# The second block's first eight rotations: halves swapped and summed by TensorE

## The reference, cut to what matters

```python
def rope(x, pos):
    half = x.shape[-1] // 2
    ...
    x1, x2 = xf[..., :half], xf[..., half:]
    return jnp.concatenate([x1 * cos - x2 * sin, x1 * sin + x2 * cos], axis=-1).astype(x.dtype)

qa = rope(qa.reshape(bsz, L, A_HEADS, HEAD_DIM), positions)   # 512 columns: rotations 4 to 7
ka = rope(ka[:, :, None, :], positions)[:, :, 0]              # rotation 3
qi = rope(qi.reshape(bsz, L, IDX_HEADS, IDX_DIM), positions)  # 256 columns: rotations 0 and 1
ki = rope(ki[:, :, None, :], positions)[:, :, 0]              # rotation 2
o_a = dsa_attention(qa, ka, va, qi, ki, wi)

# in dsa_attention, for a block of queries:
idx_logit = jax.nn.relu(jnp.einsum('bthd,bsd->bths', _rows(qi, t0), ki))
score = jnp.einsum('bth,bths->bts', _rows(wi, t0), idx_logit)
_, sel = lax.top_k(score, k_sel)                              # 256 keys, then softmax attention over them
```

## Time and profile before

| | |
|---|---|
| median of 3 runs | 2726.5 us (2716.0 to 2730.44) |
| profiled execution | 2723.89 us, its span 2722.0 us |
| busy share of the span | TensorE 87%, VectorE 62%, ScalarE 48%, GpSimd 31% |
| mean granted clock of TensorE | 0.933 of full |
| chain that ended last | TensorE 52%, VectorE 23%, ScalarE 11%, GpSimd 6%, issue 5% |
| 1 MB chunks of `in_w_in` | 5.5 us from issue to landing (median of 14) |

### The profile page before, as it was taken

One profiled execution on the slowest core, in us unless ns is written; L12 is line 12 of the kernel. 1 busy time (PEld: TensorE's weight loads), 2 busy tenths in 40 slices (PEclk: granted clock), 3 DMA queues, 4 the chain that ended last, 5 costly groups with the idle time before them and its releaser, 6 DMA issues.

```text
span 2722.0 us, 38617 instructions
## 1 busy us (share of the span) xinstructions
PE 2378.0 (87%) x15899; PEld 2119.0 (78%) x15899; DVE 1695.0 (62%) x2589; ACT 1309.9 (48%) x2133; POOL 849.3 (31%) x519
## 2 busy tenths in 40 slices
PE   4999997888899999999998886888887874999994
PEld 3999997888899889899897775667666763877773
DVE  3445545778843766666666657846566425888885
ACT  3444333344433556565565343542344212888884
POOL 1211114455431222222221124213010113776672
PEclk8999997899999999999998998898898976999997
DMA  4232420111052222222222323124111432888773
GB/s 145 78 93 79 129 78 32 32 32 32 13 143 71 64 78 79 71 75 65 76 67 55 88 64 92 47 65 115 39 43 41 126 104 90 290 284 288 277 265 146
DMA packets 228329, 275.54 MB, mean 101 GB/s; under 512 B 42792, under 2 KB 194953, under 8 KB 215482
## 3 DMA queue, kind: packets, MB, share of 16 engines
q1 hardware_dynamic: 213642, 264.64, 31.1%
q0 software_dynamic: 14512, 8.45, 1.0%
HBM read 283.24 MB, written 31.05 MB: 115 GB/s over the span
## 4 chain that ended last, share of the span: by engine, by line
PE 52%; DVE 23%; ACT 11%; POOL 6%; issue 5%; DMA 2%; SPq 1%; DVEq 0%; POOLq 0%; ACTq 0%
PE ps L92 16%; PE ps L94 14%; PE ps L93 14%; ACT whi L98 2%; DVE prods L1143 2%; DVE wlo L102 2%; ACT sp L114 1%; PE ps L1819 1%; DVE fsum L970 1%; DVE work L2682 1%; POOL wlo L102 1%; DVE m L2680 1%; DVE p L2114 1%; ACT X L114 1%; PE ps L1829 1%
## 5 line engine op out<-in xcount | busy, mean ns | idle before, releaser
L92 PE MATMUL ps<-hn_h,whi 128*128 128x264 f32 (+2 forms) x2256 | 691.6, 307 | 39.3 <-POOL wlo L102 30.0
L93 PE MATMUL ps<-hn_l,whi 128*128 128x264 f32 (+2 forms) x2256 | 674.3, 299 | 0.0
L94 PE MATMUL ps<-hn_h,wlo 128*128 128x264 f32 (+2 forms) x2256 | 674.0, 299 | 0.0
L92 PEld LDWEIGHTS ps<-hn_h,whi 128*128 128x128 f32 x2256 | 431.1, 191 | 68.4 <-issue 37.3
L94 PEld LDWEIGHTS ps<-hn_h,wlo 128*128 128x128 f32 x2256 | 431.1, 191 | 12.5
L93 PEld LDWEIGHTS ps<-hn_l,whi 128*128 128x128 f32 x2256 | 431.3, 191 | 9.5
L102 POOL TENSOR_TENSOR wlo<-wraw,whi 128x2048 fp32r<-128x2048 f32 (+1 forms) x48 | 176.8, 3683 | 508.1 <-ACT whi L98 508.1
L98 ACT ACTIVATE whi<-wraw 128x2048 fp32r<-128x2048 f32 (+1 forms) x164 | 260.1, 1586 | 64.8 <-PE ps L94 64.5
L102 DVE TENSOR_TENSOR wlo<-wraw,whi 128x2048 fp32r<-128x2048 f32 (+1 forms) x116 | 244.5, 2108 | 49.0 <-ACT whi L98 48.9
L730 DVE SCALAR_TENSOR_TENSOR c<-ub,vec,c 128x528 f32<-128x528 f32 x48 | 45.3, 943 | 140.1 <-ACT c L114 140.0
L114 ACT ACTIVATE ub<-ps,vec 128x528 f32<-128x528 f32 x48 | 33.7, 702 | 165.1 <-PE ps L94 165.1
(11 more groups left out here) (766 smaller groups left out, 6778.8 us busy)
## 6 DMA issues: line engine op xcount, KB each, us to landing
wraw<-in_w_gate_up SPq DMA_DIRECT2D x33, 1024.0 KB, 7.5
wraw<-in_hy_w_in SPq DMA_DIRECT2D x32, 1024.0 KB, 5.8
wraw<-in_da_w_in SPq DMA_DIRECT2D x64, 512.0 KB, 4.3
ex_raw<-in_w_gate_up SPq DMA_DIRECT2D x31, 1024.0 KB, 6.4
ex_raw<-in_w_down SPq DMA_DIRECT2D x17, 1024.0 KB, 6.0
wraw<-in_w_down SPq DMA_DIRECT2D x15, 1024.0 KB, 7.5
wraw<-in_w_in SPq DMA_DIRECT2D x14, 1024.0 KB, 5.5
wraw<-in_hy_w_out SPq DMA_DIRECT2D x8, 1024.0 KB, 8.5
```

Source lines behind the costliest of these rows:

```text
L92: e.matmul(out, lhsT=l[0], rhs=r[0], start=start, stop=False)
L93: e.matmul(out, lhsT=l[0], rhs=r[1], start=False, stop=False)
L94: return e.matmul(out, lhsT=l[1], rhs=r[0], start=False, stop=stop)
```

## The change

The three last weight chunks of the group change places: qa0 comes before ki. GpSimd splits ki and the last three gate chunks; VectorE splits qa0, ka, qa1 and the first gate chunk. For rotations 0 to 7 ScalarE's copy, the swaps by transfer and GpSimd's products are gone. VectorE reads the bank twice and writes the products with cosines and with sines (`vector_parts`); TensorE adds them in the same bank with two float32 matmuls, one with the identity and one with a matrix that swaps the halves and turns the sign (`tensor_rotation`). High and low parts of 3 to 7 are made from the bank; 0 to 2 are multiplied by the norm out of the bank. Turns 0 to 2 stand inside projection 4, the others behind projections in `MIX`. Banks are free when a rotation's low part is done. The index scores have five banks and not six. Rotations 8 to 13 stay.

```diff
     plan("vgw", cols(mw, (576, 640, 0), (2216, 2240, 64), (928, 936, 88)))
     plan("qi", wk(mw, (640, 896)))
+    plan("qa0", wk(mw, (0, 256)))
     plan("ki", cols(mw, *[(896, 928, 32 * i) for i in range(4)]))
     plan("ka", cols(mw, (512, 576, 0), (512, 576, 64)))
-    plan("qa0", wk(mw, (0, 256)))
     plan("qa1", wk(mw, (256, 512)))
...
-        pool = i in even_slots if i >= EX else i % 3 == 0 and i != DAO + 1 or first["gate", "a", 0] <= i < first["cmp"]
+        pool = i in even_slots if i >= EX else i % 3 == 0 and i != DAO + 1
+        if first["vgw"] <= i < first["cmp"]:
+            pool = i == first["ki"] or i > first["gate", "a", 0]
         return ("w.lo.pool", i) if pool and not gathered(i) else ("w.lo.vec", i)
...
+        for i, g in enumerate((32, 16)):
+            to, by = (x.rearrange("p (a h r) -> p a h r", h=2, r=g) for x in (swaps[:, i, :], ident[:]))
+            for h in range(2):
+                ts(e, to[:, :, h, :], by[:, :, 1 - h, :], -1.0, None, ALU.mult).then_inc(*mark("dao.pool", "swaps"))
         for m in range(8):
             lo_weights(e, w, "pool", first["dao", m] + 1 if m < 7 else first["ki"])
...
     def left(w, x):
 
-        w.wait_ge("px.act" if x < 9 else "px.vec", "left", x)
+        if x == 0:
+            w.wait_ge("px.act", "left", 0)
+        elif x < 9:
+            w.wait_ge("px.vec", "turned", PX[x][2])
+        else:
+            w.wait_ge("px.vec", "left", x)
 
     def px_bank(x):
-        return bank[3 + x] if x < 3 else bank[(x + 1) % 2]
+        return bank[3 + x] if x < 3 else bank[x % 3] if x < 9 else bank[(x + 1) % 2]
...
     def tensor_project(e, w, x):
-        if x == 4:
-            w.wait_ge("dao.vec", "evicted", 7, 0)
+        if x < 6:
+            w.wait_ge("dao.vec", "evicted", 7, x - 4)
+        elif x < 9:
+            left(w, x - 3)
+        elif x < 11:
+            w.wait_ge("at.act", "exp", 14, 1)
         else:
             left(w, x - 2)
-        if x in (9, 10):
-            w.wait_ge("at.act", "exp", 14, 1)
         for k in range(8):
             if (x, k) == (4, 0):
                 w.wait_ge("n2.vec", "acc")
                 w.wait_ge("n2.pool", "acc")
                 tensor_columns(e, sq8b[:, 0], range(4)).then_inc(*mark("n2.pe", "sum"))
-            if (x, k) == (4, 3):
+            if x == 4 and k in (3, 5, 6):
+                tensor_rotation(e, w, k // 2 - 1 if k < 6 else 2)
+            if (x, k) == (4, 4):
                 w.wait_ge("n2.vec", "r")
                 tensor_along(e, bank[7], by_n2, range(4)).then_inc(*mark("n2.pe", "r"))
             tensor_project_part(e, w, x, k)
 
+    def vector_parts(e, w, rot):
+
+        x = rotated_at[rot]
+        hi, lo, tab, scale, _ = ROT[rot]
+        came(w, x)
+        if rot < 3:
+            tables_there(w)
+        else:
+            w.wait_ge("n2.vec", "table", tab + 1)
+        if rot >= 4:
+            w.wait_ge("px.pe", "turn", rot - 4)
+        for i, y in enumerate(turning(rot)):
+            t = (tabs if rot < 3 else tabs_r)[:, tab + i, :]
+            e.scalar_tensor_tensor(y[:], px_bank(x), scale, t, ALU.mult, ALU.mult).then_inc(*mark("px.vec", "parts", rot))
+
+    def tensor_rotation(e, w, rot):
+        b = px_bank(rotated_at[rot])
+        c, s = turning(rot)
+        w.wait_ge("px.vec", "parts", rot)
+        w.wait_ge("dao.pool", "swaps")
+        e.matmul(b, lhsT=ident[:], rhs=c[:], start=True, stop=False)
+        e.matmul(b, lhsT=swaps[:, ROT[rot][2] // 2, :], rhs=s[:], start=False, stop=True).then_inc(*mark("px.pe", "turn", rot))
...
     def scalar_project(e, w, x):
         name, c, rot, over = PX[x]
-        b = px_bank(x)
         if x > 3:
             scalar_weights(e, w, first[name] + 1)
-        if x < 9:
+        if x == 0:
             came(w, x)
-        if x == 0:
-            act(e, vg[0:96, :], b[0:96], ACT.Copy).then_inc(*mark("px.act", "left", x))
-        elif x < 9:
-            turning_free(w, rot, "turned")
-            act(e, turning(rot)[0][:], b, ACT.Copy, scale=ROT[rot][3]).then_inc(*mark("px.act", "left", x))
-        elif rot is not None and ROT[rot][4]:
+            act(e, vg[0:96, :], px_bank(0)[0:96], ACT.Copy).then_inc(*mark("px.act", "left", x))
+        elif x > 9 and rot is not None and ROT[rot][4]:
...
     def scalar_rotated(e, w, rot):
-        w.wait_ge("px.vec", "rotated", rot)
+        if 3 <= rot < 8:
+            w.wait_ge("px.pe", "turn", rot)
+            src = px_bank(rotated_at[rot])
+        else:
+            w.wait_ge("px.vec", "rotated", rot)
+            src = turning(rot)[0][:]
...
-        elif rot is not None:
-            g = 32 if ROT[rot][2] == 0 else 16
-            r, s, _ = turning(rot)
+        elif rot is not None and rot >= 8:
+            r, s = turning(rot)
             left(w, x)
-            turning_free(w, rot, "rotated")
-            for j in range(128 // g):
-                e.dma_start(s[g * j:g * j + g, :], r[g * (j ^ 1):g * (j ^ 1) + g, :]).then_inc(*land(f"rot{rot % 4}", rot))
...
     def vector_rotated(e, w, rot):
         hi, lo = ROT[rot][0:2]
-        r, s, _ = turning(rot)
+        r, s = turning(rot)
+        b = px_bank(rotated_at[rot])
         if rot < 3:
-            w.wait_ge("px.vec", "sum", rot)
+            w.wait_ge("px.pe", "turn", rot)
             w.wait_ge("n2.act", "r")
-            e.scalar_tensor_tensor(r[:], r[:], 1.0, rr2[:], ALU.mult, ALU.mult).then_inc(*mark("px.vec", "rotated", rot))
-        else:
+            e.tensor_tensor(r[:], b, rr2[:], ALU.mult).then_inc(*mark("px.vec", "rotated", rot))
+        elif rot >= 8:
             w.wait_ge("px.pool", rot)
             add(e, r[:], r[:], s[:]).then_inc(*mark("px.vec", "rotated", rot))
         w.wait_ge("px.act", "turned", rot)
-        lo_sum(e, lo, r[:], hi).then_inc(*mark("px.vec", "turned", rot))
+        if 3 <= rot < 8:
+            lo_part(e, lo, b, hi).then_inc(*mark("px.vec", "turned", rot))
+        else:
+            lo_sum(e, lo, r[:], hi).then_inc(*mark("px.vec", "turned", rot))
...
     def index_bank(i, h):
-        return bank[2 + (8 * i - 8 + h) % 6][:, 0:128 * (i + 1)]
+        return bank[3 + (8 * i - 8 + h) % 5][:, 0:128 * (i + 1)]
...
-    MIX = [("px", 4), ("first", 0), ("first", 1), ("rot", 0), ("vg",), ("px", 5), ("first", 2), ("rot", 1), ("rot", 2), ("tables",),
-           ("px", 6), ("ix", 1, 0), ("ix", 1, 1), ("rot", 3), ("px", 7), ("rot", 4), ("ix", 2, 0), ("ix", 2, 1), ("px", 8), ("rot", 5),
-           ("ix", 3, 0), ("ix", 3, 1), ("rot", 6), ("rot", 7)]
+    MIX = [("px", 4), ("vg",), ("rot", 0), ("rot", 1), ("rot", 2), ("tables",), ("parts", 3), ("ix", 1, 0), ("ix", 1, 1),
+           ("px", 5), ("turn", 3), ("rot", 3), ("parts", 4), ("px", 6), ("turn", 4), ("rot", 4), ("ix", 2, 0), ("ix", 2, 1), ("parts", 5),
+           ("px", 7), ("turn", 5), ("rot", 5), ("ix", 3, 0), ("ix", 3, 1), ("parts", 6), ("px", 8), ("turn", 6), ("rot", 6), ("parts", 7),
+           ("turn", 7), ("rot", 7)]
 
     def sync_mix(e, w):
-        for x in range(1, 4):
-            sync_project(e, w, x)
...
@@ -2752,11 +2782,8 @@
                     scalar_p1_root(e, w, 1)
                 if (z, k) == (0, 4):
                     scalar_weights(e, w, first["ka"])
-                if (z, k) == (1, 3):
-                    scalar_weights(e, w, first["qa0"])
+        scalar_project(e, w, 0)
         scalar_weights(e, w, first["qa1"])
-        for x in range(4):
-            scalar_project(e, w, x)
...
         mix_tree(e, w, "n2.vec", 1, add)
+        vector_parts(e, w, 0)
         w.wait_ge("n2.act", "sqrt")
         e.reciprocal(by_n2, by_n2).then_inc(*mark("n2.vec", "r"))
-        lo_weights(e, w, "vec", first["qa0"])
+        vector_parts(e, w, 1)
+        vector_parts(e, w, 2)
+        lo_weights(e, w, "vec", first["qa1"])
...
     def gpsimd_mix(e, w):
         mix_tree(e, w, "n2.pool", 0, lambda e, out, a, b: e.tensor_tensor(out, a, b, ALU.add))
-        lo_weights(e, w, "pool", first["qa1"])
-        for x in range(1, 4):
-            gpsimd_project(e, w, x)
         for kind, *of in MIX:
             if kind == "px":
...
+            w.wait_ge("px.vec", "turned", 3)
             w.wait_ge("px.vec", "turned", 4 + a)
             w.wait_ge("ix.act", 3, 7)
             mask = selb[:, i - 1, 0:nk] if i else trir[:]
@@ -2939,7 +2967,9 @@
             w.wait_ge("px.vec", "turned", 12 if z == "slc" else 13)
             mask = trir[:]
         if n == 0:
+            left(w, 6)
             left(w, 7)
+        elif n == 1:
             left(w, 8)
         elif n == 16:
             left(w, 17)
```

More of the change, by code:

```diff
@@ L2177, in build @@
     aside.append([sb(f"aside4{x}", [128, 1024], F32R, A + 83968 + 4096 * j) for j, x in enumerate("hl")])
+    swaps = sb("swaps", [128, 2, 128], F32, A + 24576 + 3392)
     aside.append([sb("aside5h", [128, 1024], F32R, A + 61952), sb("aside5l", [128, 1024], F32R, A + 40960)])
@@ L2510, in sync_project @@
```

(48 more changed lines are left out.)

17 lines of the change are left out of this document (7 added, 10 removed).

## The result

The changed kernel takes 2728.0 us (median of 20 runs, 2722.2 to 2736.7), the kernel before 2720.9 (20 runs, 2716.0 to 2730.4): a ratio of 1.0027, 95% interval 1.0018 to 1.0037. That is 7.1 us more, against 6 forecast, and inside half a per cent. The profiled execution took 2732.8 us, its span is 2730.8, its mean granted clock 0.934.

A forecast was written before the change was run, and what follows sets the result against it. In the 79.6 us stretch of eight rotations it took VectorE as first candidate, with nothing full. Part A +4.5, part B +1.2 and the attention's start +0.3 gave +6 on 2723.9: 2730 us, range 2719 to 2742.

The forecast's parts named there:

- Part A: Ahead of the rotations, ki loads later, delaying squares, sum and projection tail: +4.5 us (3.0 to 4.7).
- Part B: Rotations, tree to first attention maximum: GpSimd interference removed, turns and waits added: +1.2 us (-0.4 to +2.9).
- ki's wait for VectorE's split of vgw and for its transfer: Ahead of the last projection's end, ki arrives at 1591.6, so squares of tile (7, 0) start 2.75 us late.
- GpSimd's part meets the sum: GpSimd's split of ki, some 2.3 us alone, meets VectorE's sum of squares again; the sum is 3.0 us late.
- The half clock: Projection tail after TensorE's wait: 3.4 us of work at half clock, costing 1.5 us (bounds 0 and 1.7).
- What GpSimd had cost VectorE: Rotation stretch: some 13 us of VectorE time removed (tree 4.2, index 1 4.9, the add 2.8, others).
- The price of the turn: Two 512-column float32 matmuls on TensorE per rotation: 1.65 us at full clock, 3.3 at half (bounds 0.5 and 6.6).
- the signs that I had set: Wrong if ki split at once, turns over 2.7, or first maximum after first projections over 4 us off 76.5.
- (1) ki in time: At the chunk reordering, ki lands sooner and only qa0's 1.7 us is added there: 2727 or 2724; chance 0.2.
- (2) The turn is dear: Float32 turns on TensorE cost 3.3 us each, 11.5 more: 2741, deciding from 2.7 a turn; chance 0.13.
- (3) Slow steps not GpSimd's doing: Index 1's 4.9 us and the tree's 4.2 stay on VectorE: 2739; chance 0.04.
- rival 4: VectorE's queue doesn't idle at the turns, some 20 us of idling fall away: 2710; chance 0.05.

The follow-up runs named there:

- experiment 1: Changed kernel with the weight chunks back in their old order, ki before qa0: 2725.1 us, ratio 1.0009.
- (2): Kernel before the change with only the new chunk order, qa0 ahead of ki: 2725.5 us, ratio 1.0019.
- Experiment 3: Changed kernel with sixteen matmuls nobody reads on TensorE ahead of its wait for the sum of squares: 2728.6 us, ratio 1.0029.
- Experiment 4: Changed kernel with each turn's two float32 matmuls issued twice, same result: 2750.4 us, ratio 1.0107.
- 8: Changed kernel with old chunk order, top-k ahead of lows, vg behind rotation 2, and qa1's and first gate chunk's low parts on GpSimd: 2714.2 us, ratio 0.9975.
- 5: Changed kernel with VectorE's three top-k steps ahead of the low part of rotations 3 to 7: 2721.4 us, ratio 1.0006.
- 6: Changed kernel with vg moved behind rotations 0 to 2 in the order: 2723.6 us, ratio 1.0012.
- experiment 7: Changed kernel with ki ahead of qa0, top-k steps ahead of the lows of rotations 3 to 7, vg behind rotations 0 to 2: 2709.5 us, ratio 0.9953.

## Why the prediction came out as it did

The size, 7.1 us against 6, the mechanism and the place were right. But in the profiles both parts, A (the late chunk) and B (the rotations), are dearer than forecast: at the first maximum the changed kernel is 11.2 and 10.4 us late in the two pairs. That 2730 lies within 2 us of the 2728.0 measured is in part luck, as the sum below shows.

**Part A, forecast +4.5, measured +6.6 and 7.1 at the first normalised tile.** The mechanism is shown twice, by taking the order out (1) and by putting it alone into the old kernel (2). Its steps:

- ki's wait for VectorE's split of vgw and for its transfer: the squares of (7, 0) 3.1 late (2.75 forecast). VectorE's split ended where I had it, 2.85 after tile 6; ki's split on ScalarE began 0.4 later than I had worked out.
- GpSimd's part meets the sum: 2.34 and 2.39 beside each other. The 2.3 that I had from 3.55 less 1.3 fits. The sum is 3.6 late (3.0 forecast).
- The half clock is the mis-sized term: 3.0 and not 1.5. I had let it end after 3.4 us, as in the earlier trace rows; here the mean over the 8 us of the tail was 0.59, some 6.6 us at the lower level. Experiment 3 gives 2.5 to 3.0 of it back, with nothing changed but the sixteen matmuls.

**Part B with the attention's start, forecast +1.5, measured +4.4 and 3.1.** Stretch by stretch on VectorE, forecast and measured in the changed kernel, each up to the event named, worked out from the timeline:

```
tree                                   2.4    2.4
vg begins                             13.5   14.4
index 1 done                          14.7   14.8
rotation 3 done                        4.8    5.8
rotation 4 done                        7.2    7.4
index 2 done                           8.6    8.6
rotation 5 done                        4.2    4.6
index 3 done                           9.7    9.6
rotation 6 done                        4.2    4.6
rotation 7 done                        8.7    9.2
first maximum of the attention         3.1    2.7
sum                                   81.1   84.1
```

- What GpSimd had cost VectorE was priced rightly: tree and index steps to within 0.1 us. Where VectorE works through its own queue, the forecast holds to 0.1. The 0.3 for the attention's start didn't come: the first maximum follows the last top-k step without a wait, although the window from 1716 to 1720 is at 0.50.
- What is off are the six stretches that end at a turn: 0.9, 1.0, 0.2, 0.4, 0.4 and 0.5. The price of the turn is the smaller part of this. It is 1.72 and 3.7, not 1.65 and 3.3, some 0.9 over the eight; I had scaled it from float32 matmuls of 128 columns, and within its bounds of 0.5 and 6.6 that was near. Of the 0.9 ahead of vg, 0.7 is that TensorE ended the first projections at 1639.85, 3.75 after the tree began, where I had 3.1. At rotations 4 and 6 VectorE waits 2.71, where my prices (1.65, and 0.7 for the high part) give 2.35: ScalarE begins its high part 2.0 us after the turn begins. The 1.0 at rotation 3 is mostly the half clock behind the 7.57 us idle time, for which I had allowed 1. The windows there:

```profile
1660.40:1664.00 3.60, 2.57 (x26) 1.99 (x27) 3.27 (x7) 1.70 (x6) 0.00 (x0) 0.50 0.00 0
1664.00:1668.00 4.00, 4.00 (x15) 3.19 (x14) 3.12 (x7) 1.05 (x3) 0.00 (x0) 0.74 0.00 0
```

  They read half clock for 3.6 us and for about half of the next 4. The Trainium skill, "TensorE: Matmul & The Clock Gate", section "HAM oscillation", says that a burst behind a wait starts at half rate each time. The trace agrees at the three longest waits of this stage (4.24, 5.43 and 7.57 us, each with 0.50 behind it), and not at the shorter one ahead of turn 5 (2.55, with 1.00 behind it). Its reading was nearer than mine for part A: 4.7 against 4.5, with 6.6 measured, since most of the tail ran at half clock.

By the signs that I had set, the forecast passed narrowly. The first maximum comes 80.3 us after the end of the first projections, 3.8 off the old 76.5, where more than 4 was to mean wrong. With ki first (experiment 1) it is 82.8.

**The sum.** In the profiles the two errors are on one side, and 10.4 to 11.2 would have given 2731 to 2732 on a median of 2720.9. The median moved by 7.1 (4.9 to 10.1 by the interval). Part of the gap is that part A isn't the same in every execution. Five profiles run the changed code unaltered as far as the tree (the changed kernel twice, every turn twice, top-k ahead, vg last). The tree stands at 49.8, 50.2, 47.9, 47.9 and 49.9 there: 4.8 to 7.2 us late. Behind an idle time of 3.36 us ahead of the first projections, the same in all five, TensorE has a second stretch at half clock in some and not in others. These are the windows from 22 to 28 us after tile 6, of the changed kernel and of the one with top-k ahead:

```profile
1608.30:1614.30 6.00, 4.87 (x23) 4.90 (x24) 2.11 (x6) 1.63 (x4) 0.00 (x0) 0.50 0.00 0
```
```profile
1604.20:1610.20 6.00, 3.39 (x28) 3.33 (x28) 3.23 (x10) 1.90 (x5) 0.00 (x0) 1.00 0.00 0
```

Both profiles of the changed kernel have the dearer form. How often it comes in the twenty runs isn't recorded, so it may account for some 2 of the 3 to 4 us between profiles and medians, and the rest stays open. The other explanation is that later stages give some back. Experiment 4 speaks against it: 18.9 in the stage became 22 at the end. From the end of attention a to the end of the program the twelve profiles take 901 to 911 us, without any order by how late they are; but the changed kernel's two (901 and 904) do lie below the two of the kernel before (905 and 909), and two pairs can't settle it. The forecast of 2730 was also set on a profiled execution that lay 3.0 above the final median of before. The rise itself was forecast 1 us too small by the medians and 4 to 5 too small by the profiles.

**The rivals.** (1) ki in time: refuted by the 2.93 us wait. (2) The turn is dear: not at full clock, 1.72 against the 2.7 from which it decides; at half clock (turn 7) it is. Experiment 4 has turns of 3.4 and shows what they would have done: 2750, where I had 2741, since more turns then begin at half clock. (3) Slow steps not GpSimd's doing: refuted by 2.40 and 4.03, and by 8, where a GpSimd split lying over a mask add made it 4.52. The Trainium skill's "SBUF — State Buffer", section "Who interferes with whom", has both halves of this: two SBUF inputs contend, one doesn't; the trace has 4.52 for the first and 0.68 for the second. (4) VectorE's queue doesn't idle: refuted for this order by 22 us of waits, but 5, 6 and 7 show that most of it is a matter of order. Behind each wait stood work in the same queue that needed nothing of what was waited for: the top-k steps, and rotations 0 to 2. With that work moved ahead, 8 us of waits are left in experiment 7 of the 22. That it then takes the 2710 that rival 4 had named is in part chance, since experiment 7 also takes back part A, which rival 4 had left in.

So the change traded some 13 us of VectorE time behind GpSimd for round trips of VectorE, TensorE and ScalarE, and wrote them down so that VectorE stood still in most of them; and it moved the four-piece chunk so far back that ScalarE's queue has to wait for its transfer.
